# Three gate stages of a decoder trunk: gate steps in pairs at every second block, their banks emptied in the same block, their stores one block earlier

## The chip, the cores and the metric

The kernel runs on one core of one Trainium2 chip. The metric is the device time of one execution in microseconds (us); the median of three runs of the kernel before is 1455.04 us (1454.61 to 1455.71). The chip's matrix engine is PE in the profile (PEld is its weight load), the vector engine DVE, the scalar engine ACT, the general engine POOL, and SP is the engine that issues most DMAs.

## What is computed

The reference is one layer of a hybrid decoder trunk over 512 tokens of width 1024. After a mixer of three groups of heads comes the part that this case is about, a retrieval over 16384 single-neuron experts:

```python
scores = jnp.einsum("thcd,hcnd->thcn", q, keys)
s_top, i_top = lax.top_k(scores, PEER_TOPK)          # 16 of 128, two halves of the key
...
best, pos = lax.top_k(cand, PEER_TOPK)               # 16 experts of each of 8 heads
gates = jax.nn.softmax(best, axis=-1)
...
act = jax.nn.gelu(jnp.einsum("thkd,td->thk", u_tab[ib], xb), approximate=False)
w = gb * act
return jnp.einsum("thk,thkd->td", w, v_tab[ib])
```

## The kernel before

Tokens 128 to 511 (three tiles of 128) are computed densely: for each of 128 blocks of 128 experts, PE makes the activations of all 384 tokens (`up`), and later the sum over experts (`down`). What the routing picked is turned into a dense matrix of gates, experts by tokens, that multiplies the activations. The first 128 tokens go another way: each picks 128 experts (8 heads by 16), POOL fetches their rows of `u` (and later of `v`) in 128 gathers, each one row of 4 KB for each of the 128 tokens, 512 KB, and DVE takes the dot products (`dot`, one for each gather).

The first pass runs over blocks i = 0 to 127. Block i needs:

- SP: `load_u`, 512 KB into one of four slots of `uraw`, issued in SP's iteration i-4, after DVE's `lower_u` of block i-4 has freed the slot (L396 to L400);
- ACT: `upper_u(i)` rounds it to `uhi` (L1447), two blocks ahead of PE; DVE: `lower_u(i)` makes the rest, `ulo` (L1841);
- PE: `up`, 24 matmuls of 384 columns, 16 on `uhi` and then 8 on `ulo`, into one of two banks;
- ACT: `activations(i)`, the Gelu that empties the bank (L1454); PE's block i+2 waits for it. SP stores it, 192 KB (`store_act`, L377).

Three gate stages lie inside this pass, one for each tile of tokens, in the 16 blocks that begin at `HOT_AT` = 20, 56 and 92 (h below is such a first block). A gate step n (0 to 15) turns 8 tokens into columns of the gate matrix:

- DVE: `one_hot(n)` makes `hotA`, `hotB` and `hotLo` (L2002 to L2005), in two buffers. The buffer of step n is free when PE has done gate step n-2;
- ACT: `weigh(n)`, 8 instructions, makes `hotHi` from `hotA` (L1475), also in two buffers;
- PE: `gates(n)`, 16 matmuls of 128 columns in float16, into one of two pairs of banks;
- ACT: `stage_gates(n)` empties the pair into `stage` (L1486); four steps fill a chunk, of which there are two buffers;
- SP: `store_gates` writes a chunk in four parts of 512 KB, one in each of four iterations (L383, L393). `stage_gates` of the first step of a chunk waits until the chunk two before it is stored.

In a gate stage PE's order was gates(n), up(h+n) for n = 0 to 15. ACT's order in its block i = h+n was `upper_u(i+2)`, `stage_gates(n-1)`, `activations(i-1)`, `weigh(n+1)`. DVE's was `one_hot(0)` and then for each n: `lower_u(h+n)`, `one_hot(n+1)`, and one or two dots (one and two by turns in the first two stages, two in the third). All engines' orders are written out by hand; each queue of instructions is in order, and the semaphores only make it wait. After the third stage PE goes on with blocks 108 to 127, ACT, DVE and SP with it, and then the second pass (`down`, L1110) begins.

Of the kernel before, what the change touches and what calls it, by code (L numbers as in the profile page):

```python
# [82 lines left out]
HOT_AT = [20, 56, 92]  # L83
# [17 lines left out]
CPT = P // CHUNK_T  # L101
CHUNKS_G = TD // CHUNK_T
# [60 lines left out]
def trunk(nc, xT_d, x_d, memT_d, wch_d, wv_d, par_d, dtb_d, alog_d, g2row_d, wout_d, wq_d, keys_d,  # L163
# [5 lines left out]
    with ctx:  # L169
# [155 lines left out]
        def _(sp):  # L325
# [64 lines left out]

            def load_g(e, g):
                sp.dma_start(gring[:, e], gates_d[:, :, bass.ds(4 * g, 4), :]).then_inc(g_in[e], 16)
            chunk_at = {HOT_AT[c // CPT] + 4 * (c % CPT) + 3 + part: (c, part) for c in range(CHUNKS_G) for part in range(4)}  # L393
            for k in range(4):
                load_u(k, k)
            for i in range(NK - 4):  # L396
# [8 lines left out]
                k, now = divmod(i - FIRST_DOWN, 3)  # L405
# [134 lines left out]
        def _(pe):  # L540
            def mm(out, lhsT, rhs, start=True, stop=True, shared=False):
                return nc.tensor.matmul(out, lhsT, rhs, start=start, stop=stop, skip_group_check=shared)  # L542
# [316 lines left out]
            for i in range(2):  # L859
                pe.wait_ge(s["sqym_ready"], i + 1)  # L860
                last = mm(o, ones[:], sq[:, i, :], i == 0, i == 1)
            done(last, "ssqym")
            o = job("ssqy")
            for i in range(SC):
                pe.wait_ge(s["sqy_ready"], i + 1)
                last = mm(o, ones[:], cin[:, i, 0:T], i == 0, i == SC - 1)
# [144 lines left out]
            def key_scores(t):  # L1011

                pe.wait_ge(s["sco_ready"], 4 * t)
                if t > 1:
                    pe.wait_ge(s["g_free"], 16 * (t - 2) + 2)
                for h in range(PH):
                    if t == 1:
                        pe.wait_ge(s["pq_ready"], PH - 1 + h // 4)
                    for c in range(2):
                        r_ = slice(HD * c, HD * (c + 1))  # L1020
                        last = mm(psum[:, 4 + 2 * c + h // 4, (h % 4) * P:(h % 4 + 1) * P],
                                  pqT[r_, h, (t - 1) * P:t * P], keysT[r_, h, :])
                        if h % 4 == 3:
                            last.then_inc(s["sco_full"], 1)

            def up(k, i):

                pe.wait_ge(s["uhi_ready"], i + 1)

                pe.wait_ge(s["act_ready"], i + 1)  # L1030
                out = psum[:, k % 2, 0:TD]
                for c in range(DC):
                    mm(out, uhi[:, k, c, :], hhi[:, c, :], c == 0, False)
                    mm(out, uhi[:, k, c, :], hlo[:, c, :], False, False)
                pe.wait_ge(s["u_split"], i + 1)
                for c in range(DC):
                    last = mm(out, ulo[:, k, c, :], hhi[:, c, :], False, c == DC - 1)
                last.then_inc(s["p1_done"], 1)
# [10 lines left out]
            def gates(tt, q, n):  # L1049

                k, a = n % 2, HOT_AT[tt] // 4
                step = 4 * q + (16 * tt - 4 * a + n + 1)
                pe.wait_ge(s["hotLo_ready"], step)
                pe.wait_ge(s["hotHi_ready"], step)

                pe.wait_ge(s["g_free"], step)
                for i in range(8):
                    o = psum[:, 4 + 2 * k + i // 4, (i % 4) * P:(i % 4 + 1) * P]
                    b = hotB[:, k, i // 2, :, i % 2]
                    mm(o, b, hotHi[:, k, i, :], True, False)  # L1060
                    last = mm(o, b, hotLo[:, k, i // 2, :, i % 2], False, True)
                last.then_inc(s["g_full"], 1)

            def ups(a, b):
                if a // 4 < b // 4:
                    with pe.Fori(a // 4, b // 4) as q:
                        for k in range(4):
                            up(k, 4 * q + k)
                for i in range(b // 4 * 4, b):
                    up(i % 4, i)  # L1070
# [10 lines left out]
            for t in range(1, NT):  # L1081
                a, h = ROUTE_AT[t], HOT_AT[t - 1]
                if t < NT - 1:
                    ups(a, h - 4)
                    key_scores(t + 1)
                    ups(h - 4, h - 2)
                else:
                    ups(a, h - 2)
                turned(t - 1)
                up((h - 2) % 4, h - 2)  # L1090
                up((h - 1) % 4, h - 1)
                pe.wait_ge(s["sco_ready"], 4 * min(t + 2, NT))
                with pe.Fori(h // 4, h // 4 + 4) as q:
                    for k in range(4):
                        gates(t - 1, q, k)
                        up(k, 4 * q + k)
            ups(REST_AT, NK - 4)

            pe.wait_ge(s["g_free"], 16 * DT + 2)
# [27 lines left out]
        def _(act):  # L1127
# [309 lines left out]
            def softmax(t):  # L1437
                act.wait_ge(s["soft_in"], t + 1)
                a_(sm[:, 1], sm[:, 0], ACT.Exp).then_inc(s["soft_out"], 1)
                act.preload_act_table(ACT.Gelu)  # L1440
# [29 lines left out]
            def weigh(n):  # L1470

                act.wait_ge(s["hotA_ready"], n + 1)
                for i in range(8):
                    token = 8 * (n % 16) + i
                    ins = a_(hotHi[:, n % 2, i, :], hotA[:, n % 2, i // 2, :, i % 2], ACT.Copy, scale=ghi[:, token:token + 1])  # L1475
                ins.then_inc(s["hotHi_ready"], 1)

            def stage_gates(n):

                k, c = n % 2, n // 4  # L1480
                act.wait_ge(s["g_full"], n + 3)
                if n % 4 == 0 and c >= 2:

                    act.wait_ge(gate_stored[c % 2], 64 * (c // 2))
                by_key = psum[:, 4 + 2 * k:6 + 2 * k, :].rearrange("p b (t i) -> p i (b t)", t=4)
                a_(stage[c % 2][:, :, 8 * (n % 4):8 * (n % 4) + 8], by_key, ACT.Copy, scale=1.0 / GATE_SCALE).then_inc(s["g_free"], 1)  # L1486
# [13 lines left out]
            for i in range(NK - 4):  # L1500
                if i in softs:
                    softmax(softs[i])
                for tt in range(DT):
                    n = i - HOT_AT[tt]
                    if n == -1:
                        if tt + 2 < NT:
                            for m in range(PH // 2):
                                key_scores(tt + 2, m)
                        routed_turned(tt)
                if early <= i + AHEAD < NK:  # L1510
                    upper_u(i + AHEAD)
                for tt in range(DT):
                    n = i - HOT_AT[tt]
                    if 0 < n <= 16:
                        stage_gates(16 * tt + n - 1)
                if i:
                    activations(i - 1)
                for tt in range(DT):
                    n = i - HOT_AT[tt]
                    if -1 < n + 1 < 16:  # L1520
                        weigh(16 * tt + n + 1)

            for e in range(2):
                act.wait_ge(gate_stored[e], 64 * (CHUNKS_G // 2))
# [23 lines left out]
        def _(dve):  # L1548
# [432 lines left out]
            def hot(tt):  # L1981

                if tt == 0:
                    link(v.tensor_copy(iota2[:], iota128[:].unsqueeze(2).broadcast_to([P, P, 2])))
                dve.wait_ge(s["rT_ready"], tt + 1)

                link(v.tensor_copy(halves16[:, 0, :], gate[:]))
                link(v.tensor_copy(ghi[:], halves16[:, 0, :]))
                link(v.tensor_tensor(halves16[:, 1, :], gate[:], ghi[:], ALU.subtract))

                def one_hot(n):

                    e, step = n % 2, 16 * tt + n + 1
                    tokens = slice(8 * n, 8 * n + 8)

                    dve.wait_ge(s["g_full"], step)

                    keys2 = iota2[:].unsqueeze(1).broadcast_to([P, 4, P, 2])

                    def each_key(row):  # L2000
                        return row[:, tokens].rearrange("p (j r) -> p j r", r=2).unsqueeze(2).broadcast_to([P, 4, P, 2])
                    v.tensor_tensor(hotA[:, e], keys2, each_key(idx[:, 0, :]), ALU.is_equal).then_inc(s["hotA_ready"], 1)  # L2002
                    v.tensor_tensor(hotB[:, e], keys2, each_key(idx[:, 1, :]), ALU.is_equal)
                    dve.wait_ge(s["hotA_ready"], step)
                    v.tensor_tensor(hotLo[:, e], hotA[:, e], each_key(halves16[:, 1, :]), ALU.mult).then_inc(s["hotLo_ready"], 1)  # L2005
                one_hot(0)
                for n in range(16):
                    up_to(HOT_AT[tt] + n + 1, 0)
                    if n < 15:
                        one_hot(n + 1)  # L2010
                    up_to(0, dotted[0] + (2 if tt == DT - 1 else 1 + n % 2))
            residual(0)
            residual(1)
# [121 lines left out]
```

## Time and profile before

| | before |
|---|---|
| median of 3 runs | 1455.04 us |
| the profiled execution | 1454.85 us |
| its span, first to last instruction | 1453.1 us |
| PE busy | 1435.0 us (99%) |
| DVE busy | 1161.5 us (80%) |
| ACT busy | 699.9 us (48%) |
| POOL busy | 325.3 us (22%) |
| DMA, whole span | 403.04 MB, 277 GB/s |

The span is what lies between the first and the last instruction on the core; 1.75 us lie around it. Busy shares are means over a program with several stages, and a busy PE may still be slower than it could be; what a change is worth has to be read in the stage that it touches.

### The profile page before, as it was taken

The page shows a single profiled execution, that of the slowest core. Times are in us where ns is not written, and L with a number is a line of the kernel's source. Part 1 is how long each engine was busy: PE and PEld are TensorE (multiplying, and loading weights), DVE is VectorE, ACT ScalarE, POOL GpSimd, SP SyncE. Part 2 cuts the span into 40 slices and gives each one's busy share as a digit, 9 for nine tenths or more (in the row PEclk, how much of TensorE's full clock was granted, in tenths as well). Part 3 has the DMA queues.
Part 4 walks back from the last instruction along what each step waited for, and adds up shares of the span by engine and source line. Part 5 has one row for each costly group of instructions (what it writes and reads, how often), then busy time and mean ns, then how long its engine had stood idle before and what let it go on. Part 6 is the DMA issues. An engine that isn't in the chain of part 4 may idle for free.

```text
span 1453.1 us, 23528 instructions
## 1 busy us (share of the span) xinstructions
PE 1435.0 (99%) x7901; PEld 1249.8 (86%) x7901; DVE 1161.5 (80%) x2215; ACT 699.9 (48%) x1238; POOL 325.3 (22%) x300
## 2 busy tenths in 40 slices
PE   8999989999999999999999999999999999999998
PEld 5887756589999999999999999888888888888887
DVE  6655573989989999899999963798788788888885
ACT  5454673134469833896359833443333333333331
POOL 1000200024023212232125512343322222322210
PEclk9999999999999999999999999999999999999999
DMA  7120304058579986799779999899999999999993
GB/s 304 46 72 2 145 1 174 1 219 301 194 244 351 403 297 223 271 391 384 246 255 366 418 392 362 324 364 354 352 354 346 339 329 363 335 376 347 355 347 144
DMA packets 175764, 403.04 MB, mean 277 GB/s; under 512 B 14672, under 2 KB 96592, under 8 KB 175184
## 3 DMA queue, kind: packets, MB, share of 16 engines
q1 hardware_dynamic: 138832, 268.02, 50.7%
q0 software_dynamic: 36864, 134.23, 25.5%
q8 instruction: 28, 0.46, 0.1%
q14 instruction: 40, 0.33, 0.1%
HBM read 347.67 MB, written 54.53 MB: 277 GB/s over the span
## 4 chain that ended last, share of the span: by engine, by line
PE 91%; DVE 5%; DMA 1%; ACT 1%; issue 1%; SPq 0%; DVEq 0%; ACTq 0%
PE psum L542 55%; PE psum L1110 36%; DMA uraw<-in_uT 1%; DVE sco L1908 0%; DVE x L1719 0%; DVE itop L1912 0%; DVE itop L1906 0%; DVE x L1811 0%; DVE h2row L1821 0%; DVE pr L1747 0%; DVE top L1904 0%; DVE top L1910 0%; DMA wring<-in_chunks 0%; DVE mstat L1754 0%; ACT pr L1298 0%
## 5 line engine op out<-in xcount | busy, mean ns | idle before, releaser
L542 PE MATMUL psum<-hhi,uhi 128*128 128x384 f32 x1024 | 348.1, 340 | 1.6 <-ACT act_s L1454 1.6
L542 PE MATMUL psum<-hlo,uhi 128*128 128x384 f32 x1024 | 342.5, 334 | 0.0
L1533 ACT ACTIVATE vhi<-vraw 128x1024 fp32r<-128x1024 f32 x128 | 135.9, 1062 | 311.0 <-PE psum L1110 291.0
L516 POOL DMA_INDIRECT urow<-in_u,eidx x128 | 162.6, 1270 | 507.1 <-DVE urow L1847 357.4
L1110 PE MATMUL psum<-vhi,wlo 128*128 128x512 f32 x768 | 236.6, 389 | 0.0
L1110 PE MATMUL psum<-vhi,whi 128*128 128x512 f32 x768 | 236.5, 389 | 0.1
L1110 PE MATMUL psum<-vlo,whi 128*128 128x512 f32 x768 | 236.4, 389 | 0.0
L516 POOL DMA_INDIRECT urow<-in_v,eidx x120 | 138.6, 1155 | 375.3 <-DVE acc L2068 374.7
L2062 DVE TENSOR_TENSOR vlo<-vraw,vhi 128x1024 fp32r<-128x1024 f32 x128 | 156.4, 1222 | 61.3 <-ACT vhi L1533 61.2
L542 PE MATMUL psum<-hhi,ulo 128*128 128x384 f32 x1024 | 198.3, 334 | 0.0
L542 PEld LDWEIGHTS psum<-hhi,uhi 128*128 128x128 f32 x1024 | 192.3, 188 | 2.7 <-ACT uhi L1447 2.2
L542 PEld LDWEIGHTS psum<-hlo,uhi 128*128 128x128 f32 x1024 | 192.4, 188 | 0.1
L1841 DVE TENSOR_TENSOR ulo<-uraw,uhi 128x1024 fp32r<-128x1024 f32 x128 | 156.0, 1221 | 38.3 <-ACT uhi L1447 36.0
L542 PEld LDWEIGHTS psum<-hhi,ulo 128*128 128x128 f32 x1024 | 179.3, 188 | 0.0
L1110 PEld LDWEIGHTS psum<-vhi,wlo 128*128 128x128 f32 x768 | 144.2, 188 | 30.0
L1110 PEld LDWEIGHTS psum<-vhi,whi 128*128 128x128 f32 x768 | 144.1, 188 | 30.0 <-issue 0.4
L1110 PEld LDWEIGHTS psum<-vlo,whi 128*128 128x128 f32 x768 | 144.2, 188 | 29.8
L2068 DVE SCALAR_TENSOR_TENSOR acc<-urow,wrow,acc 128x1024 f32<-128x1024 f32 x128 | 163.4, 1277 | 0.0
L1847 DVE SCALAR_TENSOR_TENSOR urow<-urow,h2row 128x1024 f32<-128x1024 f32 x128 | 153.1, 1218 | 4.6 <-DMA urow<-in_u,eidx 4.4
L1447 ACT ACTIVATE uhi<-uraw 128x1024 fp32r<-128x1024 f32 x128 | 135.3, 1057 | 43.5 <-DMA uraw<-in_uT 43.4
L1454 ACT ACTIVATE act_s<-psum 128x384 f32<-128x384 f32 x128 | 62.6, 489 | 180.5 <-PE psum L542 164.5
L1475 ACT ACTIVATE hotHi<-hotA,ghi 128x128 f16<-128x128 f16 x384 | 117.3, 393 | 0.0
(302 smaller groups left out, 1789.7 us busy)
## 6 DMA issues: line engine op xcount, KB each, us to landing
uraw<-in_uT SPq DMA_DIRECT2D x128, 512.0 KB
vraw<-in_v SPq DMA_DIRECT2D x128, 512.0 KB
acts_scratch<-act_s SPq DMA_DIRECT2D x128, 192.0 KB
gates_scratch<-stage SPq DMA_DIRECT2D x48, 512.0 KB
gring<-gates_scratch SPq DMA_DIRECT2D x32, 768.0 KB
aring<-acts_scratch SPq DMA_DIRECT2D x128, 192.0 KB
wring<-in_chunks SPq DMA_DIRECT2D x18, 512.0 KB, 5.0
wout<-in_wout SPq DMA_DIRECT2D x1, 4096.0 KB, 12.6
```

What stands on the lines that cost most here:

```text
L516: g.indirect_dma_start(urow[k], None, table, bass.IndirectOffsetOnAxis(eidx[:, n % HK:n % HK + 1], 0)).then_inc(row_in[k], 16)
L542: return nc.tensor.matmul(out, lhsT, rhs, start=start, stop=stop, skip_group_check=shared)
L1110: last = nc.tensor.matmul(psum[:, 2 + 2 * t + half, :], l_[:, k, t * P:(t + 1) * P], r_[:, k, half * 512:(half + 1) * 512], start=fresh an ...
L1447: a_(uhi[:, i % 4], uraw[:, i % 4], ACT.Copy).then_inc(s["uhi_ready"], 1)
L1454: a_(act_s[:, i % 4, :], psum[:, i % 2, 0:TD], ACT.Gelu).then_inc(s["act_ready"], 1)
L1475: ins = a_(hotHi[:, n % 2, i, :], hotA[:, n % 2, i // 2, :, i % 2], ACT.Copy, scale=ghi[:, token:token + 1])
L1533: a_(vhi[:, k, :], vraw[:, k, :], ACT.Copy).then_inc(s["vhi_ready"], 1)
L1841: v.tensor_tensor(ulo[:, k], uraw[:, k], uhi[:, k].bitcast(F32), ALU.subtract).then_inc(s["u_split"], 1)
L1847: v.scalar_tensor_tensor(urow[k], urow[k], 1.0, h2row[:, 0, :], ALU.mult, ALU.mult, accum_out=dots[:, j:j + 1]).then_inc(s["dot_ready"], 1)
L2062: v.tensor_tensor(vlo[:, k, :], vraw[:, k, :], vhi[:, k, :].bitcast(F32), ALU.subtract).then_inc(s["v_split"], 1)
L2068: v.scalar_tensor_tensor(acc0[:], urow[ROW_SLOT[r]], wrow[:, bass.ds(i, 1)], acc0[:], ALU.mult, ALU.add).then_inc(s["vrow_free"], 1)
```

## The change

PE keeps gates(0), up(h) at the start of a gate stage, then takes the gate steps in pairs: gates(1), gates(2), up(h+1), up(h+2), gates(3), gates(4), up(h+3), up(h+4) and so on, up to gates(13), gates(14), up(h+13), up(h+14), gates(15), up(h+15). The loop runs three times instead of four, and its last turn is written out. ACT's order in block i = h+n is now `upper_u(i+2)`, `activations(i-1)`, `stage_gates(n)`, `weigh(n+2)`; in the first block of a stage `weigh(1)` comes ahead of the activations. DVE makes `one_hot(0)` and `one_hot(1)` ahead of the stage, and then for each n `lower_u(h+n)`, `one_hot(n+2)`, dots. SP stores each part of a chunk one iteration earlier.

```diff
-            chunk_at = {HOT_AT[c // CPT] + 4 * (c % CPT) + 3 + part: (c, part) for c in range(CHUNKS_G) for part in range(4)}
+            chunk_at = {HOT_AT[c // CPT] + 4 * (c % CPT) + 2 + part: (c, part) for c in range(CHUNKS_G) for part in range(4)}
...
-                with pe.Fori(h // 4, h // 4 + 4) as q:
-                    for k in range(4):
+                def gate_steps(q, last):
+
+                    up(0, 4 * q)
+                    for k in (1, 3):
                         gates(t - 1, q, k)
+                        if not (last and k == 3):
+                            gates(t - 1, q, k + 1)
                         up(k, 4 * q + k)
+                        if k == 1:
+                            up(2, 4 * q + 2)
+                gates(t - 1, h // 4, 0)
+                with pe.Fori(h // 4, h // 4 + 3) as q:
+                    gate_steps(q, False)
+                gate_steps(h // 4 + 3, True)
...
                 for tt in range(DT):
-                    n = i - HOT_AT[tt]
-                    if 0 < n <= 16:
-                        stage_gates(16 * tt + n - 1)
+                    if i == HOT_AT[tt]:
+                        weigh(16 * tt + 1)
                 if i:
                     activations(i - 1)
                 for tt in range(DT):
                     n = i - HOT_AT[tt]
-                    if -1 < n + 1 < 16:
-                        weigh(16 * tt + n + 1)
+                    if 0 <= n < 16:
+                        stage_gates(16 * tt + n)
+                    if n == -1 or 0 <= n < 14:
+                        weigh(16 * tt + (0 if n == -1 else n + 2))
...
                 one_hot(0)
+                one_hot(1)
                 for n in range(16):
                     up_to(HOT_AT[tt] + n + 1, 0)
-                    if n < 15:
-                        one_hot(n + 1)
+                    if n < 14:
+                        one_hot(n + 2)
                     up_to(0, dotted[0] + (2 if tt == DT - 1 else 1 + n % 2))
```

## Rows read from the trace of the kernel before

**Rows 1.** The page, busy time, share and instructions of each engine.

```profile
PE 1435.0 (99%) x7901; PEld 1249.8 (86%) x7901; DVE 1161.5 (80%) x2215; ACT 699.9 (48%) x1238; POOL 325.3 (22%) x300
```

**Rows 2.** Waits of PE, 330 to 914 us: total, times, longest (us).

```profile
PE psum L542 <- ACT act_s L1454: 1.6, 2, 0.8
```

**Rows 3.** Timeline of PE (start us, us, instruction): gate steps and plain blocks.

```profile
422.78 0.23 PE L542 MATMUL psum<-hotHi,hotB 128*128 128x128 f16 x1
...
479.68 0.22 PE L542 MATMUL psum<-hotLo,hotB 128*128 128x128 f16 x1
...
480.47 0.22 PE L542 MATMUL psum<-hotLo,hotB 128*128 128x128 f16 x1
...
500.28 0.23 PE L542 MATMUL psum<-hotHi,hotB 128*128 128x128 f16 x1
...
563.68 0.33 PE L542 MATMUL psum<-hhi,uhi 128*128 128x384 f32 x1
...
567.84 0.33 PE L542 MATMUL psum<-hhi,uhi 128*128 128x384 f32 x1
```

**Rows 4.** The tile hotLo: durations in ns, shortest, median, longest.

```profile
L542 PEld LDWEIGHTS psum<-hotLo,hotB x384: 96/96/108, 422.8 to 836.1; 128*128 128x128 f16 x192
```

**Rows 5.** Timeline of ACT, third stage: its first weigh, then one later block.

```profile
753.82 2.44 ACT L1475 ACTIVATE hotHi<-hotA,ghi 128x128 f16<-128x128 f16 x8
...
778.65 2.45 ACT L1475 ACTIVATE hotHi<-hotA,ghi 128x128 f16<-128x128 f16 x8
780.99 1.05 ACT L1447 ACTIVATE uhi<-uraw 128x1024 fp32r<-128x1024 f32 x1
781.94 1.01 ACT L1486 ACTIVATE stage<-psum 128x1024 f32<-128x1024 f32 x1
783.43 0.49 ACT L1454 ACTIVATE act_s<-psum 128x384 f32<-128x384 f32 x1 [0.48 <-PE psum L542]
```

**Rows 6.** Timeline of DVE over one block of the third gate stage.

```profile
758.93 0.68 DVE L2002 TENSOR_TENSOR hotA<-iota,idx 128x1024 f16<-128x1024 f16 x1
...
760.74 1.22 DVE L1847 SCALAR_TENSOR_TENSOR urow<-urow,h2row 128x1024 f32<-128x1024 f32 x1
...
763.03 1.22 DVE L1841 TENSOR_TENSOR ulo<-uraw,uhi 128x1024 fp32r<-128x1024 f32 x1
764.17 0.68 DVE L2002 TENSOR_TENSOR hotA<-iota,idx 128x1024 f16<-128x1024 f16 x1
```

**Rows 7.** Windows: length, busy (instructions) by engine, clock, DMA share, GB/s.

```profile
753.69:774.36 20.67, 20.67 (x162) 20.04 (x161) 20.67 (x33) 18.85 (x48) 9.02 (x7) 1.00 0.88 301
774.36:779.53 5.17, 5.17 (x42) 5.01 (x41) 5.17 (x9) 4.69 (x13) 2.56 (x3) 1.00 0.91 308
779.53:784.70 5.17, 5.17 (x42) 5.01 (x41) 5.17 (x9) 4.69 (x13) 2.56 (x3) 1.00 0.99 383
784.70:862.20 77.50, 75.65 (x537) 73.36 (x536) 64.37 (x96) 54.08 (x119) 33.82 (x26) 1.00 1.03 417
438.50:500.50 62.00, 62.00 (x484) 60.11 (x482) 57.22 (x97) 56.38 (x133) 23.21 (x20) 1.00 0.99 377
```

**Rows 8.** Timeline of ACT and PE where the third stage ends, idle time in brackets.

```profile
826.32 1.03 ACT L1486 ACTIVATE stage<-psum 128x1024 f32<-128x1024 f32 x1 [2.94 <-DMA gates_scratch<-stage]
...
830.15 0.22 PE L542 MATMUL psum<-hotHi,hotB 128*128 128x128 f16 x1 [0.26 <-issue]
...
849.71 0.41 PE L542 MATMUL psum<-hhi,uhi 128*128 128x384 f32 x1 [0.76 <-ACT act_s L1454]
...
853.36 1.06 ACT L1447 ACTIVATE uhi<-uraw 128x1024 fp32r<-128x1024 f32 x1 [3.79 <-DMA uraw<-in_uT]
...
854.94 0.41 PE L542 MATMUL psum<-hhi,uhi 128*128 128x384 f32 x1 [0.82 <-ACT act_s L1454]
```

**Rows 9.** Timeline of SP: the stage's first store, and chunk 1's last.

```profile
779.15 0.43 SPq L383 DMA_DIRECT2D gates_scratch<-stage  x1
...
815.32 0.45 SPq L383 DMA_DIRECT2D gates_scratch<-stage  x1
```

## The prediction, made before the changed kernel ran

> **What bounds the kernel now.** I read first the page's busy shares: PE is at work 99% of the span, every other engine 80% or less [rows 1], so time can only come out of PE's own stream or out of the little it waits. Next PE's waits over the first pass: two waits for a drained bank, 1.6 us in all [rows 2], and one late gate step [rows 8]. So inside the three gate stages PE is dense, and the question is how fast its stream goes there. Its timeline says: the first gate step of stage 1 starts at 422.78 and the sixteenth at 500.28, 15 blocks in 77.50 us, 5.167 us for one gate step and one block of `up`. A plain block takes 567.84 - 563.68 = 4.16 us, and inside a gate step the matmuls follow each other every (480.47 - 479.68) / 14 = 0.0564 us, 0.90 us for 16 [rows 3]. 4.16 + 0.90 = 5.06 us: 0.10 us of each block is the price of going from one kind of matmul to the other and back.
>
> Then the windows with the DMA columns: in the third stage the DMA share climbs from 0.88 over 0.91 and 0.99 to 1.03, and stays there at 417 GB/s from 784.70 to 862.20, while in stage 1 it is 0.99 at 377 GB/s [rows 7]. In that full stretch lie all three places where PE stops: 0.26 us before the step at 830.15 (ACT had stood 2.94 us for the stores of `stage`), 0.76 us at 849.71 and 0.82 us at 854.94 (ACT's `activations` stood behind `upper_u`, which waited for its 512 KB load) [rows 8]. By starts each is 0.16 us longer, since a matmul is drawn 0.33 us long where the next may start after 4.16 / 24 = 0.17 [rows 3]: 0.4, 0.9 and 1.0 us. So DMA, not PE, sets the time at the end of stage 3.
>
> **PE's order.** The old order changes kind 16 times there and back in a stage, the new one 9 times (step 0, seven pairs, step 15). Seven round trips fewer in each of three stages, 21 x 0.10 = 2.1 us, 0.7 us a stage. Both operands of this are differences of rows of one timeline; the bounds are 0 (the second step of a pair loses what the change saves) and 0.13 us a round trip (rounding of the rows). The loop's last turn, written out, and its three turns instead of four cost nothing that I can find: blocks before and after the loop's jumps take the same 5.167 us. I take 2.1.
>
> **ACT.** The new order adds and removes no instruction. In a block ACT works 5.16 - 0.48 = 4.68 us: 2.34 for `weigh`, 0.95 for `upper_u`, 1.0 for `stage_gates`, 0.4 for `activations` [rows 5]. Two blocks are 9.4 us against PE's new 2 x 5.167 - 0.10 = 10.2. Walk one pair, steps 1 and 2, from its start at 0: PE ends them at 0.9 and 1.8, up(h+1) at 6.0, up(h+2) at 10.2. ACT empties step 1 until 1.9, weighs step 3 until 4.3, rounds until 5.2, waits for up(h+1) to 6.0, Gelu until 6.4, empties step 2 until 7.4, weighs step 4 until 9.8. Step 4 starts at 10.2 + 0.9 = 11.1, 1.3 us later. So emptying at once puts the bank's wait nowhere near PE. The tight place is the entry: from the first `weigh` at 753.82 ACT does 2.34 + 0.95 + 2.34 + 0.4 + 1.0 + 2.4 = 9.4 us until step 2 is weighed, and PE wants it 0.90 + 5.17 us after step 0, which starts at about 830.15 - 0.4 - 14 x 5.167 = 757.4, so 9.65 us after 753.82. It fits by 0.2 us; if not, 0 to 0.3 us a stage. I take 0.
>
> **DVE.** No work added, but `one_hot(n+2)` now waits for gates(n), where `one_hot(n+1)` waited for gates(n-1): in the queue behind it stand the dots and `lower_u` of the next block. In stage 3 the dots of n = 1 began at 760.74, so those of n = 0 a period of 764.17 - 758.93 = 5.24 us earlier, at 755.5 [rows 6]. Now they stand behind `one_hot(2)`, which starts when gates(0) is done, 757.4 + 0.9 + 0.2 = 758.5, and takes 760.74 - 758.93 = 1.81: 760.3, which is 4.8 us later. PE does not feel that directly: `lower_u(h+2)` ends at 1.1 + 1.81 + 2.29 + 1.14 = 6.3 us after its pair starts, and up(h+2) reaches its `ulo` part at 6.0 + 2.8 = 8.8. DVE needs 10.48 us for two blocks and PE 10.2, so this 2.5 us shrinks by 0.25 a pair and lasts for the seven pairs. In stages 1 and 2, with 1.5 dots, DVE needs 4.7 us a block and keeps up.
>
> **The stores and loads.** Each part of a chunk goes into SP's queue one iteration earlier. What is moved past: behind a first part, which now waits about 1 us longer in its iteration for `stage_gates`, SP's next `load_u` stands, and that waits for DVE until later anyway: 0. The wait of ACT for a chunk's stores: chunk 1's last part was issued at 815.32 and ACT went on at 826.32, 11.0 us [rows 8, 9]. In the new order this part goes out about 5.5 us sooner against its stage, and ACT wants it 4.7 us sooner for PE's sake. The 0.4 us at 830.15 should go.
>
> Now the full stretch. All loads and stores of SP stand in one queue, the gathers in another. Per block it is 512 (`load_u`) + 192 (Gelu) + 512 (gates) + 2 x 512 KB (gathers), 2.29 MB, 5.5 us at 417 GB/s, against 5.07 us of PE. What sets PE's late steps is when the load of block 112 lands (853.36); up(111) starts 1.58 us later, at 854.94. Three things shift this landing. One more store part stands ahead of every load until the last chunk is out: 524288 B / 417 GB/s = +1.25 us. DVE's dots, and so the gathers that they release, come 4.8 us later at two in 5.24 us: 1.8 gathers x 1.25 = 2.3 us less is moved before the engines are full, and has to be moved later. And the first store, at 779.15 [rows 9], moves into time that was partly idle: (0.12 + 0.04) x 5.17 / 1.03 = 0.8 us back. Together +2.7 us if all the gathers are through by then, +1.5 if one is still out; I take +2.1, measured from the start of the stage. So stage 3 ends 2.1 us later against its start than before: its own 0.7 us and the 0.4 us are absorbed by PE waiting longer at the same places. What recovers it? Nothing: behind it PE is dense again.
>
> In stages 1 and 2 the engines move 377 of 417 GB/s, with one dot and two by turns, so a load queue empties in each block and their 2 x 0.7 us stand.
>
> **The sum.** -1.4 + 2.1 = +0.7 us on the profiled execution of 1454.85 (span 1453.1), 1455.6. The median of the runs lies 0.19 us above that execution: 1455.7.
>
> **Weighed against the skill.** Within a gate step the rows give 0.0564 us a matmul [rows 3]. The Trainium skill ("TensorE: Matmul & The Clock Gate", section Back-to-back issue gap) gives a sustained 81 ns a matmul for a stream of weight load and matmul pairs at 128 columns, against about 56 alone, and speaks of a queue of 64 instructions. By it a pair of steps, 64 instructions, could fall from the fast pace to the slow one; worked out from its figure, an estimate, the second step of 21 pairs would cost 21 x 16 x 0.0246 = 8.3 us, and the time would be 1463.9; it is the first rival below at the page's price. The trace of before has no run longer than 16 such matmuls, and in those the pace does not fall.
>
> **The rivals.** *The supply of PE runs dry in a pair* (slower). Mechanism: 16 short matmuls live on instructions fetched under the long ones; 32 don't. Price by the nearest row: a weight load lasts 96 ns [rows 4]; if the second step went at that pace, 16 x 0.040 = 0.63 us a pair, 13.3 in all, 1454.85 - 1.4 + 2.1 + 13.3 = 1469; at a third of that 1460. It decides from 6 ns a matmul on, where 0.10 us is gone. For it: no long run in the trace. Against it: the spacing at the end of a step is that of its start. Chance 4%.
>
> *Stage 3 couples to DMA early* (slower). DVE's lag leaves `load_u` 4.8 us less time to land; if ACT and PE wait from the eighth block and not from the seventeenth, each of eight blocks costs 5.5 - 5.07 = 0.43 us more, 3.4 us: 1459.1. It decides if loads land over about 9 us after issue; the store above took 11.0. Against it: with loads issued later, less stands ahead of them. Chance 15%.
>
> *The gathers' lag is worth what the extra store costs*: landing shifts by 0 to 0.7, PE's stalls eat just the saving of stage 3: 1454.85 - 1.4 + 0.3 = 1453.8, and 1454.0 on the median. Chance 25%.
>
> *The stores' earlier start dissolves the stalls* (faster): -2.1 us and the three lateness terms, 0.4 + 0.9 + 1.0: 1454.85 - 4.4 = 1450.5. For it: the last part leaves a block sooner. Against it: the full stretch is ruled by bytes. Chance 11%.
>
> *The change does nothing to PE's stream* (round trips cost the same in total): 1457. It is inside the range.
>
> **How the numbers follow.** Forecast 45%, its own range 1454.5 to 1457.0. Measurements of this kernel tell 0.2%, 2.9 us, from no change. Faster than 1452.1: the fourth rival and a little of the third, 0.12. Slower than 1457.9: the first, most of the second and a little of the forecast, 0.17. Within: 0.71. The range 1451.8 to 1459.2 leaves 0.1 outside on each side.
>
> **What would show it.** PE's timeline: starts of pairs 10.23 us apart in stages 1 and 2, steps 3, 5, ... without a gap inside a pair. ACT: `stage` at 826 without its 2.9 us wait. The windows: 1.03 from about 780 on. PE's stops after up(108) longer than 0.76 and 0.82 us, 4 us or more together. Wrong if those stops are gone, if the second step of a pair is spaced above 0.06 us, or if PE already stops inside stage 1 or 2.

## The result, and the profile of the changed kernel

| | before, same runs | changed |
|---|---|---|
| median | 1455.49 us (1454.43 to 1457.88) | 1459.88 us (1457.98 to 1461.22) |
| the profiled execution | 1454.85 us | 1461.22 us |
| its span | 1453.1 us | 1459.5 us |

The ratio is 1.0033, with a 95% interval of 1.0025 to 1.0041: 3.6 to 6.0 us slower, clear of the 0.2% that can be told from no change. The forecast was 1455.7, with a range up to 1459.2. The profiled execution is the slowest of the ten, 1.3 us above their median, so what follows shows the loss at its largest.

The page of the changed kernel, busy time of each engine, beside [rows 1]: no engine has noticeably more work.

```profile
PE 1436.9 (98%) x7901; PEld 1254.6 (86%) x7901; DVE 1162.3 (80%) x2215; ACT 700.3 (48%) x1238; POOL 327.7 (22%) x300
```

The timeline of PE in the changed kernel (start us, us, instruction), beside [rows 3].

```profile
422.93 0.23 PE L542 MATMUL psum<-hotHi,hotB 128*128 128x128 f16 x1
...
428.10 0.23 PE L542 MATMUL psum<-hotHi,hotB 128*128 128x128 f16 x1
...
429.87 0.22 PE L542 MATMUL psum<-hotLo,hotB 128*128 128x128 f16 x1
...
438.33 0.23 PE L542 MATMUL psum<-hotHi,hotB 128*128 128x128 f16 x1
...
499.73 0.23 PE L542 MATMUL psum<-hotHi,hotB 128*128 128x128 f16 x1
...
756.16 0.23 PE L542 MATMUL psum<-hotHi,hotB 128*128 128x128 f16 x1
```

Pairs start 438.33 - 428.10 = 10.23 us apart, and the 32 matmuls of one pair start over 1.77 us, 57 ns apart, to the last one. The first stage lasts 76.80 us to the start of its last step where it lasted 77.50 [rows 3]. The third stage starts at 756.16, 1.24 us before its old 757.4, though the first one began 0.15 later: the two stages kept 1.4 us. Up to here the change did what it was to do.

Then the waits of PE, 415 to 925 us (total, times, longest), beside [rows 2].

```profile
PE psum L542 <- ACT hotHi L1485: 3.1, 1, 3.1
PE psum L542 <- ACT act_s L1464: 2.6, 2, 2.3
```

And PE's timeline at the two large stops, the idle time in brackets.

```profile
806.43 0.26 PE L542 MATMUL psum<-hotHi,hotB 128*128 128x128 f16 x1 [3.09 <-ACT hotHi L1485]
...
808.84 0.52 PE L542 MATMUL psum<-hhi,uhi 128*128 128x384 f32 x1
809.16 0.52 PE L542 MATMUL psum<-hlo,uhi 128*128 128x384 f32 x1
...
859.00 0.41 PE L542 MATMUL psum<-hhi,uhi 128*128 128x384 f32 x1 [2.29 <-ACT act_s L1464]
```

The first stop is the second step of a pair, step 10 of stage 3, waiting for its one-hot weights. It is followed by something that no number of the prediction had: matmuls 320 ns apart (809.16 - 808.84), where their pace is 173. The windows (length, busy by engine, granted clock, DMA share, GB/s) tell why: behind the first stop TensorE runs at half its clock, 1.2 GHz, and so it does from 1.1 us after the second.

```profile
806.29:811.40 5.11, 4.97 (x27) 5.00 (x27) 5.11 (x8) 4.84 (x13) 2.62 (x2) 0.50 1.04 420
857.46:862.57 5.11, 3.57 (x14) 3.60 (x15) 2.37 (x3) 1.40 (x2) 0.00 (x0) 0.76 1.02 414
```

**The account of the profiled execution.** From the stage's start to the first matmul of the next phase PE takes 6.34 + 1.24 = 7.6 us more than before (that matmul starts at 919.88, before at 913.54). The stops add, over PE's usual pace, 3.25 us at step 10, 2.46 at 859.00 and 0.48 at 915; the half clock adds about 2.7 us behind the first (matmuls of both kinds) and 1.6 behind the second. Together 10.5, less the stage's own saving of 0.7 and the 2.3 us of stops that before had here [rows 2, 8]: 7.5. So about 40% of what this stage adds is clock, not waiting. That holds for this execution, whose mean granted clock is 0.995; the nine others have 0.997 to 1.000, and the one with 1.000 still took 1458.56 us. So the waits make the change slower even without the clock.

**What was late.** ACT's timeline, from two blocks ahead of step 10 on, and then behind the stage.

```profile
793.66 1.06 ACT L1457 ACTIVATE uhi<-uraw 128x1024 fp32r<-128x1024 f32 x1 [1.79 <-DMA uraw<-in_uT]
...
799.62 1.06 ACT L1457 ACTIVATE uhi<-uraw 128x1024 fp32r<-128x1024 f32 x1 [1.28 <-DMA uraw<-in_uT]
...
802.98 1.02 ACT L1496 ACTIVATE stage<-psum 128x1024 f32<-128x1024 f32 x1 [1.92 <-DMA gates_scratch<-stage]
803.90 2.43 ACT L1485 ACTIVATE hotHi<-hotA,ghi 128x128 f16<-128x128 f16 x8
...
850.64 1.06 ACT L1457 ACTIVATE uhi<-uraw 128x1024 fp32r<-128x1024 f32 x1 [5.27 <-DMA uraw<-in_uT]
857.42 1.06 ACT L1457 ACTIVATE uhi<-uraw 128x1024 fp32r<-128x1024 f32 x1 [5.34 <-DMA uraw<-in_uT]
```

PE wants step 10 at 803.2; its `weigh` starts at 803.90, behind three waits of 1.79, 1.28 and 1.92 us for loads and for the stores of chunk 0. The reason stands in the timelines of DVE and of SP.

```profile
757.28 0.69 DVE L2013 TENSOR_TENSOR hotA<-iota,idx 128x1024 f16<-128x1024 f16 x1 [1.02 <-PE psum L542]
...
759.10 1.22 DVE L1858 SCALAR_TENSOR_TENSOR urow<-urow,h2row 128x1024 f32<-128x1024 f32 x1
...
761.39 1.22 DVE L1852 TENSOR_TENSOR ulo<-uraw,uhi 128x1024 fp32r<-128x1024 f32 x1
```

```profile
762.70 0.34 SPq L372 DMA_DIRECT2D uraw<-in_uT  x1
...
788.86 0.34 SPq L372 DMA_DIRECT2D uraw<-in_uT  x1
789.25 0.45 SPq L377 DMA_DIRECT2D acts_scratch<-act_s  x1
789.75 0.47 SPq L383 DMA_DIRECT2D gates_scratch<-stage  x1
```

DVE waits for gates(0) in front of `one_hot(2)`; the two dots and `lower_u` stand behind it, and `lower_u` releases SP's next `load_u`. That load goes out 6.5 us after the stage's start (762.70 - 756.16). Before, the one of that place went out at 1.7 and then every 5.2. The last store part of chunk 0 stands behind such a load in SP's queue: issued at 789.75, 33.6 us after the start (before 37.3, so 3.7 us sooner, not 5.5), and ACT went on at 802.98, 13.2 us later. In the kernel before the same part was issued at 794.65, 1.1 us ahead of a load and not 0.9 us behind one, and ACT's wait for it ended at 804.12, after 9.5 us. And less was moved early. DMA in the first 20 us of stage 3, changed kernel and then the kernel before:

```profile
756.16:776.16 20.00, 20.00 (x169) 19.68 (x169) 18.98 (x31) 19.62 (x52) 7.86 (x6) 1.00 0.77 256
...
816.16:836.16 20.00, 20.00 (x160) 19.69 (x159) 16.60 (x25) 18.26 (x43) 8.20 (x7) 1.00 1.01 379
```

```profile
757.40:777.40 20.00, 20.00 (x158) 19.53 (x158) 20.00 (x31) 18.37 (x44) 10.48 (x8) 1.00 0.87 300
...
817.40:837.40 20.00, 19.74 (x156) 18.98 (x155) 20.00 (x31) 16.19 (x36) 11.86 (x9) 1.00 1.03 417
```

300 - 256 = 44 GB/s over 20 us is 0.88 MB, at 417 GB/s 2.1 us owed to the full stretch. In the fourth 20 us the same shows again: after the stop at step 10 the engines moved 379 GB/s, not 417, another 1.8 us.

### The profile page after: what moved, and what is told of

The parts are those of the page before. It is cut to its first block, busy times and chain, and to the rows that moved or that the text cites. A ratio compares the mean times of both kernels' runs of the same rounds, so it can differ in the third digit from the quotient of the medians.

```text
span 1459.5 us, 23501 instructions
## 1 busy us (share of the span) xinstructions
PE 1436.9 (98%) x7901; PEld 1254.6 (86%) x7901; DVE 1162.3 (80%) x2215; ACT 700.3 (48%) x1238; POOL 327.7 (22%) x300
## 4 chain that ended last, share of the span: by engine, by line
PE 84%; DVE 9%; DMA 4%; ACT 1%; issue 1%; SPq 0%; DVEq 0%; ACTq 0%
PE psum L542 48%; PE psum L1120 36%; DMA uraw<-in_uT 3%; DVE urow L1858 2%; DMA gates_scratch<-stage 1%; DVE ulo L1852 1%; DMA xT<-in_xT 0%; DVE sco L1919 0%; DVE hotA L2013 0%; DVE hotLo L2016 0%; DVE hotB L2014 0%; DVE x L1730 0%; DVE itop L1923 0%; DVE itop L1917 0%; DVE x L1822 0%
## 5 line engine op out<-in xcount | busy, mean ns | idle before, releaser
L516 POOL DMA_INDIRECT urow<-in_u,eidx x128 | 169.7, 1326 | 502.4 <-DVE urow L1858 351.1
L516 POOL DMA_INDIRECT urow<-in_v,eidx x120 | 134.0, 1117 | 380.6 <-DVE acc L2080 380.0
```

Of the source, the lines that this page charges most:

```text
L516: g.indirect_dma_start(urow[k], None, table, bass.IndirectOffsetOnAxis(eidx[:, n % HK:n % HK + 1], 0)).then_inc(row_in[k], 16)
```

## The experiments

The profile shown of each is one execution; where it lies far from the median, the text says so. Each was timed beside the kernel before, whose median was 1454.82 us in the first four, 1455.61 in the next four and 1455.47 in the last four; ratios are to it. Theory L: the time is lost because VectorE's wait makes the loads, and with them the stores, late (from the fifth kernel on, the gathers too). Theory B: the extra store part ahead of each load. Theory F: the third stage asks for more DMA than there is, so what TensorE saves is waited off.

**The stores one block back**, all else as changed.

```diff
-chunk_at = {HOT_AT[c // CPT] + 4 * (c % CPT) + 2 + part: ...
+chunk_at = {HOT_AT[c // CPT] + 4 * (c % CPT) + 3 + part: ...
```

> The changed kernel, but the stores of a chunk begin in the iteration in which they began before. Theory L (DVE's later lower_u holds back load_u, and the loads and stores queued behind it land too late for ACT, whose stage_gates then holds up the weigh of step 10): the stores leave 5 us later still, stage_gates of step 8 waits about 7 us instead of 1.9, PE stops longer before step 10 of the third stage, and the time is 3 to 6 us above the changed kernel, about 1464. Theory B (the one more store part ahead of every load in the DMA queue is the cause): the time falls back to about 1456, the stops of PE after the third stage shrink to those of before.

1471.45 us, ratio 1.0109 (1.0092 to 1.0126). ACT's and PE's timelines:

```profile
816.12 1.02 ACT L1496 ACTIVATE stage<-psum 128x1024 f32<-128x1024 f32 x1 [8.14 <-DMA gates_scratch<-stage]
```

```profile
473.90 0.22 PE L542 MATMUL psum<-hotHi,hotB 128*128 128x128 f16 x1 [2.75 <-ACT hotHi L1485]
...
645.30 0.22 PE L542 MATMUL psum<-hotHi,hotB 128*128 128x128 f16 x1 [2.62 <-ACT hotHi L1485]
...
819.59 0.26 PE L542 MATMUL psum<-hotHi,hotB 128*128 128x128 f16 x1 [7.06 <-ACT hotHi L1485]
```

Theory L had put it at about 1464; it is 7 us above that, because PE now stops in stages 1 and 2 as well, at 473.90 and 645.30. From the start of stage 1 to that of stage 3 it takes 341.4 us (423.97 to 765.35), the changed kernel 333.2 (422.93 to 756.16): 8 of the 11 us are lost there. So a store that is late enough stops PE outside the full stretch too.

Theory B falls as the cause: without the early part the pairs lose 11 us more, and the repaired kernel below keeps the part and is faster than before. The stores' earlier start is not an extra beside the pairs, it is what they need, since ACT now wants the chunk's buffer 4.7 us sooner.

**The dots ahead of `one_hot(n+2)`.**

```diff
 up_to(HOT_AT[tt] + n + 1, 0)
+up_to(0, dotted[0] + (2 if tt == DT - 1 else 1 + n % 2))
 if n < 14:
     one_hot(n + 2)
-up_to(0, dotted[0] + (2 if tt == DT - 1 else 1 + n % 2))
```

> The changed kernel, but DVE takes the dots of a block ahead of one_hot(n+2), so that they don't stand behind its wait for gates(n). The gathers then come about 3 us sooner, the loads as late as in the changed kernel. If the gathers' lag is what costs (half of my sum in the prediction): 1 to 2 us faster than the changed kernel, about 1458. Theory L (the loads' and stores' lateness costs, not the gathers'): within 1 us of the changed kernel, or slower, since gathers take DMA time sooner. Theory B: no difference.

1456.61 us, ratio 1.0006 (0.9992 to 1.0020): by the ratios (1.0033 to 1.0006) 3.9 us of the loss are gone with the place of one line, more than either theory gave (1 to 2 us, or none). Its loads go out 2.2 us sooner than in the changed kernel, its gathers 4.3. The profile is no picture of that median: its execution took 1460.57 us, the second slowest of ten. In it there is no stop at step 10; PE stops three times behind the stage, the third time for 2.80 us at 901.03, and the clock falls behind the second and the third:

```profile
843.90 0.41 PE L542 MATMUL psum<-hhi,uhi 128*128 128x384 f32 x1 [0.85 <-ACT act_s L1464]
...
850.67 0.66 PE L542 MATMUL psum<-hhi,uhi 128*128 128x384 f32 x1 [2.37 <-ACT act_s L1464]
```

**The kernel before with VectorE's new order alone**: steps one at a time, stores at their old place.

```diff
 one_hot(0)
+one_hot(1)
 ...
-    if n < 15:
-        one_hot(n + 1)
+    if n < 14:
+        one_hot(n + 2)
```

> The kernel before (PE, ACT and SP in the old order), with DVE's new order alone: one_hot(n+2) behind the wait for gates(n), dots and lower_u behind it. Theory L: slower than before by 1 to 4 us, with stops of PE in the third stage, since loads and stores leave later against PE. Theory B: the same as before, within 0.5 us, since no store is moved.

1462.77 us, ratio 1.0054 (1.0037 to 1.0071): the order of three calls on an engine that is 80% busy costs 8 us by itself, twice what theory L gave at most. Its first 20 us of stage 3 and PE's wait at step 10 (total, times, longest):

```profile
755.91:775.91 20.00, 20.00 (x158) 19.53 (x158) 18.88 (x30) 18.36 (x44) 7.86 (x6) 1.00 0.74 241
```

```profile
PE psum L542 <- ACT hotHi L1475: 3.0, 1, 3.0
```

This is the signature of the changed kernel, bytes missing at the start and a 3 us stop in mid-stage, without pairs.

**The kernel before with ScalarE's emptying and the stores one block sooner, without pairs.**

```diff
-n = i - HOT_AT[tt]
-if 0 < n <= 16:
-    stage_gates(16 * tt + n - 1)
 ...
+if 0 <= n < 16:
+    stage_gates(16 * tt + n)
 ...
-chunk_at = {... + 3 + part: ...
+chunk_at = {... + 2 + part: ...
```

> The kernel before (PE and DVE in the old order), but ACT empties the gate banks in the same block, behind the activations, and the stores begin one iteration sooner. Theory L: no slower than before, 0 to 1 us faster, since the late step at the end of the third stage goes. Theory B: slower than before by 1 to 3 us, at the two stops of PE after the third stage.

1457.08 us, ratio 1.0014 (1.0001 to 1.0028): expected 0 to 1 us faster, measured about 2 us slower. ACT now waits for PE before emptying, 3.8 us in seven waits over stage 3, and PE stops once for 2.24 us behind the stage. Which of the two (ACT's waits or the extra store part) is the price, this run doesn't tell.

The next four ask whether the loss can be repaired, and whether the excess of DMA demand is what counts.

**`lower_u` one block ahead, and the dots ahead of `one_hot`.**

```diff
-up_to(HOT_AT[tt] + n + 1, 0)
+up_to(HOT_AT[tt] + n + 2, 0)
+up_to(0, dotted[0] + (2 if tt == DT - 1 else 1 + n % 2))
 if n < 14:
     one_hot(n + 2)
-up_to(0, dotted[0] + (2 if tt == DT - 1 else 1 + n % 2))
```

> The changed kernel with VectorE's order per gate step rewritten: lower_u runs one block further ahead, then the dots, and one_hot(n+2) last, so what it waits for (the gate matmuls of step n) has nothing of the loads or gathers behind it. Nothing else is edited. In the kernel with the dots merely put ahead (1456.61 us) load_u of the third stage went out 4.2, 9.5, 14.8 us after the stage's start; here they should go out at about -1, 4.2, 9.5, as far ahead of their stores as in the kernel before. Theory L (what costs time is that loads and gathers go out late behind VectorE's wait): no stop at step 10, the stops after the stage no larger than before's 0.76 and 0.82 us plus 0.7 us, so 1455.0 - 2.1 + 0.7 to + 1.4 = 1453.6 to 1454.3 us. Theory F (the third stage asks for 5.5 us of DMA in each 5.1 us of TensorE, and whatever TensorE saves is waited off later): the loads' lead does not matter once the engines are full, the time is that of the dots-ahead kernel, 1456.6, or at least not under 1455.

1453.41 us, ratio 0.9982 (0.9968 to 0.9997), by the ratios 7.4 us under the changed kernel, and 0.2 us off what theory L gave. The time came as said, the stops not quite: none at step 10, but behind the stage one of 2.31 us, where theory L allowed 1.5, and the clock fell 1.5 us after it (granted clock 0.66 from 845.71 to 850.71).

```profile
845.71 0.41 PE L542 MATMUL psum<-hhi,uhi 128*128 128x384 f32 x1 [2.31 <-ACT act_s L1464]
```

Its first 20 us of stage 3 move what those of before do:

```profile
756.19:776.19 20.00, 20.00 (x169) 19.68 (x169) 20.00 (x32) 19.34 (x50) 8.46 (x8) 1.00 0.86 297
```

**The same with fewer dots in stage 3** (`1 + n % 2` in all stages), **and the same edit on before and on the changed kernel.**

```diff
-up_to(0, dotted[0] + (2 if tt == DT - 1 else 1 + n % 2))
+up_to(0, dotted[0] + 1 + n % 2)
```

> The kernel with lower_u one block ahead and the dots ahead of one_hot(n+2), and in the third stage one dot and two by turns instead of two in each block; the eight dots left over are done in the blocks behind the stage, where the loop spreads them. Per block the DMA engines are then asked for 2.29 - 0.26 = 2.03 MB, 4.87 us at 417 GB/s, less than the 5.12 us of half a pair. Theory F (the excess of demand over what the engines move takes the savings): no TensorE stop inside or just behind the stage, all three stages keep 0.7 us, and the stops of before behind up(108) shrink too: 1455.0 - 2.1 - 0 to 1.6 = 1451.3 to 1452.9 us. Theory L (lateness alone): no better than the same kernel with two dots, 1453.6 to 1454.3 us. If the eight dots only move the excess into the blocks behind the stage, where ScalarE already waits for loads, the time is 1454 to 1456 us.

1456.37 us, ratio 0.9996 (0.9985 to 1.0008).

> The kernel before with one dot and two by turns in the third stage instead of two (the eight left over are done behind the stage). Control for the kernels with fewer dots. Theory F: the stops at 830.15 and behind up(108) (0.4, 0.76 and 0.82 us and what follows) come from the excess of demand in this stage, so they go: 1453 to 1454 us. If the excess is only moved behind the stage: 1455 us, no change within 0.5 us.

1459.74 us, ratio 1.0019 (1.0007 to 1.0032).

> The changed kernel with one dot and two by turns in the third stage instead of two; VectorE's order as changed, so loads and gathers still go out 4.7 us late. Theory L in its strict form (a load issued 4.7 us later lands later whatever stands in the queue): the stop at step 10 stays, 1458 to 1460 us. Theory F with lateness (lateness costs only where the queue is full): with 4.87 us of demand per 5.12 us the queue empties in each block as in stages 1 and 2, where the same lateness costs nothing; no stop at step 10, no half-clock matmuls in the stage, 1452.5 to 1455.5 us.

1460.90 us, ratio 1.0034 (1.0022 to 1.0047).

None gained. Against the same kernel with two dots the first lost 2.0 us by the ratios (0.9982 to 0.9996), the second 2.8, the third nothing. DMA in the first 20 us of stage 3, and PE behind it, in the third of them:

```profile
756.54:776.54 20.00, 20.00 (x169) 19.68 (x169) 16.89 (x26) 19.68 (x52) 4.97 (x4) 1.00 0.68 219
```

```profile
858.30 0.41 PE L542 MATMUL psum<-hhi,uhi 128*128 128x384 f32 x1 [2.34 <-ACT act_s L1464]
...
871.78 0.41 PE L542 MATMUL psum<-hhi,uhi 128*128 128x384 f32 x1 [2.35 <-ACT act_s L1464]
```

The last came out as neither theory had it: the time is above theory L's 1460, but the stops are F's. With less demand in the stage there is no stop at step 10, though the first loads go out nearly as late as in the changed kernel (5.4 and 11.7 us after the start, against 6.5 and 11.8). So loads that late don't stop PE inside the stage where less is asked of the DMA engines. They read full there too (1.03 and 417 GB/s from 795 to 800), so how much stood in the queue is not shown. But the eight dots are then fetched behind the stage, and there the same load, later by their bytes, stops PE twice, with the clock falling both times. PE also waits 1.26, 0.92 and 0.60 us for `wlo` at the start of the second pass, a wait that neither before nor the repaired kernel has; what it comes from was not followed, and it is part of the loss of the first two. My reading, argued and not shown: what counts is all that has to be moved until the last gather is through, less what was moved before the engines were full.

The last four try to separate loads from gathers, and repeat the repair.

**`lower_u` one block ahead, nothing else** (`n + 2` in the first `up_to` of the changed kernel).

> The changed kernel with lower_u one block further ahead and nothing else: the loads go out early (about -1.7, 3.0, 7.6 us after the third stage's start, as in the kernel with both edits at 1453.41 us), the gathers stay late (about 4.9, 6.4, 10.2), since the dots still stand behind one_hot(n+2). Theory L1 (the loads' lead is what costs: load_u waits for VectorE and the gates' store stands behind it in SyncE's queue): no stop at step 10, 1453 to 1455 us. Theory L2 (the gathers' lag costs: bytes not moved before the engines are full): as the changed kernel, 1458 to 1460 us. If both count, in between, 1455.5 to 1457.5.

1456.55 us, ratio 1.0008 (0.9999 to 1.0017). Loads early and gathers late is worth as much as gathers early and loads half late (1.0006). By the ratios the one takes 3.6 us off, the other 3.9, both together 7.4: both count, and within the noise (each difference is known to about 2 us) they add up. The cleanest pair is this kernel and the repaired one, timed together as the last below: with the loads early in both, gathers early or late are worth 1.0008 to 0.9986, 3.2 us, and the intervals don't meet. For the loads alone no such pair was timed together.

**Dots, `one_hot(n+2)`, then `lower_u`.**

```diff
-up_to(HOT_AT[tt] + n + 1, 0)
+up_to(0, dotted[0] + (2 if tt == DT - 1 else 1 + n % 2))
 if n < 14:
     one_hot(n + 2)
-up_to(0, dotted[0] + (2 if tt == DT - 1 else 1 + n % 2))
+up_to(HOT_AT[tt] + n + 1, 0)
```

> The changed kernel with VectorE's order dots, one_hot(n+2), lower_u: the gathers go out early (about 0.5, 1.9, 6.1 us after the third stage's start, as in the dots-ahead kernel at 1456.61 us), the loads later still than in the changed kernel, whose first ones were at 6.5, 11.8, 17.0: here about 1 to 3 us behind that. lower_u of a block is still ready for TensorE by its own sum (about 10 us after the stage's start against 10.7), with 0.3 us lost once in each stage. Theory L1 (loads): the stop at step 10 stays or comes sooner, 1460 to 1466 us. Theory L2 (gathers): 1456 to 1458 us.

1469.06 us, ratio 1.0098 (1.0083 to 1.0113). Not clean evidence for the loads: PE waited for `lower_u` itself, which I had put at 0.3 us a stage (total, times, longest, 415 to 925 us), and its third stage starts only at 762.02.

```profile
PE psum L542 <- DVE ulo L1852: 5.2, 11, 1.1
```

**The kernel before with `lower_u` one block ahead** (`n + 2` in its first `up_to`).

> The kernel before with lower_u one block further ahead in the three stages and nothing else: it separates what the repaired kernel (1453.41 us, 2 us under before) owes to its pairs and what to its earlier loads. Pairs are worth 3 x 0.7 = 2.1 us in TensorE's stream. If the earlier loads are worth nothing by themselves (in before they already lay far enough ahead of the stores): no change, 1455 to 1455.8 us. If the repaired kernel's gain is the loads' alone: 1453.4 us.

1454.46 us, ratio 0.9991 (0.9980 to 1.0002): no change that can be told.

**The repaired kernel once more.**

> The kernel with the changed kernel's pairs, lower_u one block ahead and the dots ahead of one_hot(n+2), once more beside the runs of this call, since its ratio to the kernel before, 0.9982 with an interval up to 0.9997, is near what can be told from no change. If it is faster than both kernels: ratio 0.997 to 0.999 with an interval under 1. If that was chance: an interval that takes in 1.

1454.05 us, ratio 0.9986 (0.9977 to 0.9995). It is faster than both kernels, by the ratios 2.0 us against before and 6.8 against the changed one. PE's and ACT's timelines show two stops in the stage and what they waited for:

```profile
803.49 0.22 PE L542 MATMUL psum<-hotHi,hotB 128*128 128x128 f16 x1 [0.49 <-issue]
...
826.06 0.26 PE L542 MATMUL psum<-hotHi,hotB 128*128 128x128 f16 x1 [1.94 <-issue]
```

```profile
800.03 1.02 ACT L1496 ACTIVATE stage<-psum 128x1024 f32<-128x1024 f32 x1 [1.40 <-DMA gates_scratch<-stage]
800.95 2.44 ACT L1485 ACTIVATE hotHi<-hotA,ghi 128x128 f16<-128x128 f16 x8
...
822.60 1.03 ACT L1496 ACTIVATE stage<-psum 128x1024 f32<-128x1024 f32 x1 [2.53 <-issue]
823.52 2.43 ACT L1485 ACTIVATE hotHi<-hotA,ghi 128x128 f16<-128x128 f16 x8
```

PE goes on at steps 10 and 14 each 0.1 us after `weigh` for that step ends (803.39 and 825.95), and each `weigh` stands behind a `stage_gates` that is the first of its chunk and waited 1.40 and 2.53 us. The first wait is for the stores, by the profile; the second it calls issue, and that it is for the stores of chunk 1, the last of them issued at 810.10, is my reading. So the path of the changed kernel is still there, shorter at step 10. The other profile of this same kernel, shown above, has no stop at these steps and one of 2.31 us behind the stage: which of the places stops PE changes from one execution to the next, and one profile is weak evidence that a stop is gone.

Where the 2.0 us come from can be read off the same two profiles. From the start of stage 1 to that of stage 3 both profiles take 333.2 us, before 334.6, so stages 1 and 2 keep 1.4. From the start of stage 3 to the second pass they take 158.2 and 157.0 us, before 156.1: stage 3 keeps nothing of its 0.7, as theory F had it. Against before with the same `lower_u` (0.9991) the pairs' own part, 0.0005, is not told from nothing.

## Why the prediction was wrong, step by step

**PE's order, right.** 10.23 us a pair and 0.7 us a stage, as forecast. The rival of a supply running dry did not come: 57 ns a matmul through all 32 of a pair. The Trainium skill ("TensorE: Matmul & The Clock Gate", section Back-to-back issue gap) has 81 ns sustained for such a stream; this trace doesn't agree for a run of 32.

**ACT's walk, right in its terms.** Where no transfer is late ACT keeps up, in stages 1 and 2 and to step 8 of stage 3. It had 1.3 us of margin, and its waits for DMA in the two blocks ahead of step 10 were 5.0 us.

**DVE, the step that failed.** The delay was right, the first dot 2.9 us after the stage's start (759.10 - 756.16), as reckoned (760.3 - 757.4). "PE does not feel that directly" was right too, and I stopped there. The queue behind the wait also held `lower_u`, which frees the slot of `load_u`; the prediction costed its end only against PE (6.3 against 8.8 us) and not against SP, which issues the next load with it, and the store behind that.

**Stores, wrong.** "`load_u` waits for DVE until later anyway: 0" names the very wait that grew. SP's queue is in order, so the store part went out 3.7 us sooner, not 5.5, less than the 4.7 us by which ACT wants it sooner; and it landed after 13.2 us. The 11.0 of the sum was read from chunk 1; chunk 0's last part, the one that holds up step 10, took 9.5 in before. I put the 3.7 us more down to the load that now goes out right ahead of it; no run isolates that. The kernel with the stores put back waited 8.14 us there and lost 11 us more, so ACT's wait for the stores, which the sum had only as a gain of 0.4 us, is worth several us.

**The full stretch, right in kind, short in size.** The bytes missing at its start came out as reckoned, 2.1 us against the 2.3 of the gathers. The 0.8 us of recovered idle time did not come: the share was 0.77 over those 20 us. The sum ended there, with PE waiting at the same places as before. In fact a first stop came in mid-stage, and twice a stop of over 2 us brought the clock down, in the profiled execution 4.3 us for which the sum had no term.

**The odds.** What happened is the rival "stage 3 couples to DMA early", given 15%. Its price, 1459.1, is 0.8 us from the median, though its working (0.43 us in each of eight blocks) isn't what the trace shows: one stop and a slow clock. Its condition was "if loads land over about 9 us after issue; the store took 11.0". I set it aside with "with loads issued later, less stands ahead of them". The trace doesn't bear that out: loads still went out every 5.2 us, only 4.8 us later, and chunk 0's last store took 13.2 us, not less than before. The row against it, 11.0 us [rows 8, 9], was in hand. That the price came so near is in part luck.

**The tests named in advance.** The pairs, the 2.9 us wait at 826 (gone) and the DMA share (1.03 from 780.7 on) came as said. The stops behind up(108) did not reach 4 us together, they were 2.3 and 0.3, because the larger one had come at step 10.

## What to carry to other kernels

When a wait is moved earlier in an engine's queue, list everything behind it, and follow each to what it frees: here the subtraction was in time for its reader, but the slot it freed was late for the next load. Where transfers run at the limit, bytes not moved before the limit is reached came back here as waits in it and behind it, and moving demand behind the stretch didn't shorten them. When work is paired to save a round trip, put what feeds the transfers ahead of the new wait: here these two moves in one engine's order turned 1.0033 into 0.9982 and 0.9986.

## What the runs showed of the hardware

- The clock's price. In the changed kernel TensorE fell from 2.4 to 1.2 GHz (granted clock 0.50) right behind a stop of 3.09 us, and 1.1 us after one of 2.29 had ended. Ten to thirteen 384-column matmuls then ran at 320 ns and not 173; the stop of 2.3 us cost about 4. It did not fall behind the stops of 0.76 and 0.82 us in before [rows 8].
- The length of a stop alone doesn't tell. The clock also fell behind stops of 1.94 us (the repaired kernel's second profile) and 2.06 us (`lower_u` ahead alone), and it stayed at 1.00 behind stops of 2.24 us (early stores alone), 2.06 us (VectorE's new order alone, at 859.78), and 2.75 and 2.29 us (stores put back, at 473.90 and 872.31).
- No window shown moved more than 420 GB/s. The Trainium skill ("Perfetto Trace Analysis", section Roofline) gives about 435 GB/s for one core's 16 engines, and the windows stay below it.
- At that ceiling a 512 KB store took 9.5 to 13.2 us from issue to the release of its reader. The longest had a load issued 0.9 us ahead of it.
